# Three norms of a two-block transformer kernel: tile by tile, half by half, and the indexer weights turned afterwards

## The reference

```python
xn = _rmsnorm(x, mix_norm)
lru_x, lru_gate, q, k, v, qi, ki, wi, gate_a, gate_b = _split_cols(xn @ w_in)
ya = (rg_lru(causal_dwconv(lru_x)) * gelu(lru_gate)) @ w_lru_br
wih = wi * (IDX_HEADS ** -0.5)        # 8 indexer weights per token
score = einsum('bth,bths->bts', wih, relu(dots(qi, ki)))
yb = attention(q, k, v, top 64 keys of score, rel_bias) @ w_attn_br
x = x + (sigmoid(gate_a) * ya + sigmoid(gate_b) * yb) @ w_out
xn = _rmsnorm(x, ffn_norm)
x = x + (gelu(causal_dwconv(xn @ w_up[:, :D_FF])) * (xn @ w_up[:, D_FF:])) @ w_down
g_ple = sigmoid(_rmsnorm(x, ple_norm) @ w_ple_gate)
x = x + g_ple * (p @ w_ple_proj)
```

## Time and profile before

| | us |
|---|---|
| runs, median (lowest to highest of 3) | 1819.99 (1817.11 to 1826.1) |
| the profiled execution, its own time | 1821.22 |
| its span, first to last instruction | 1819.5 |
| PE busy | 1431.4 (79% of the span) |
| POOL busy | 612.7 (34%) |
| ACT busy | 442.8 (24%) |
| DVE busy | 421.3 (23%) |
| mean granted clock of TensorE | 0.917 of full |

### The profile page before, as it was taken

One profiled execution on the slowest core, in us unless ns is written; L12 is line 12 of the kernel. 1 busy time (PEld: TensorE's weight loads), 2 busy tenths in 40 slices (PEclk: granted clock), 3 DMA queues, 4 the chain that ended last, 5 costly groups with the idle time before them and its releaser, 6 DMA issues.

```text
span 1819.5 us, 21776 instructions
## 1 busy us (share of the span) xinstructions
PE 1431.4 (79%) x9218; PEld 983.6 (54%) x9218; DVE 421.3 (23%) x883; ACT 442.8 (24%) x538; POOL 612.7 (34%) x493
## 2 busy tenths in 40 slices
PE   7999998776567657765766677565899899899997
PEld 7899985333133213321332133121798888799985
DVE  3994542000000000000000000001317444233202
ACT  3445631000000000000000000001347453544333
POOL 6895870000000000000000000002386958688892
PEclk9999998898898889888998889888799899899998
DMA  9353467999999999999999999999155343355550
GB/s 351 139 186 140 174 232 269 406 409 410 410 409 410 410 409 410 410 409 409 410 410 409 410 410 409 410 410 417 62 180 193 123 162 139 139 186 186 185 185 24
DMA packets 116579, 539.45 MB, mean 296 GB/s; under 512 B 4440, under 2 KB 8544, under 8 KB 108832
## 3 DMA queue, kind: packets, MB, share of 16 engines
q1 hardware_dynamic: 113232, 532.44, 74.9%
q0 software_dynamic: 1184, 3.94, 0.6%
q10 hardware_dynamic: 2096, 2.11, 0.4%
HBM read 537.41 MB, written 1.06 MB: 296 GB/s over the span
## 4 chain that ended last, share of the span: by engine, by line
PE 44%; DMA 41%; SPq 6%; DVE 3%; ACT 3%; POOL 2%; issue 1%; DVEq 0%; ACTq 0%
DMA ring<-in_w 40%; PE bank L562 35%; SPq L384 6%; PE bank L782 6%; POOL ring_parts L499 2%; ACT ring_parts L1027 1%; DVE rows_parts L1803 1%; PE bank L768 0%; DMA ring<-in_units 0%; PE bank L695 0%; DVE slab L1830 0%; PE bank L740 0%; PE bank L817 0%; PE bank L959 0%; ACT slab L1187 0%
## 5 line engine op out<-in xcount | busy, mean ns | idle before, releaser
L499 POOL TENSOR_TENSOR ring_parts<-ring,ring_parts 128x512 fp32r<-128x512 f32 x456 | 598.6, 1351 | 160.7 <-ACT ring_parts L1027 160.7
L782 PE MATMUL bank<-ring,slab 128*32 128x512 f32 x2016 | 335.5, 801 | 291.7 <-DMA ring<-in_w 290.8
L562 PE MATMUL bank<-slab_parts,ring_parts 128*128 128x256 f32 x3328 | 500.8, 285 | 10.9 <-POOL ring_parts L499 8.4
L562 PEld LDWEIGHTS bank<-slab_parts,ring_parts 128*128 128x128 f32 x3328 | 460.0, 194 | 15.5 <-POOL ring_parts L499 8.8
L782 PEld LDWEIGHTS bank<-ring,slab 128*32 128x32 f32 x2016 | 66.3, 133 | 560.1 <-DMA ring<-in_w 371.5
L514 POOL TENSOR_TENSOR slab_parts<-slab,slab_parts 128x1088 fp32r<-128x1088 f32 x1 | 2.5, 2485 | 946.1 <-ACT slab_parts L1177 946.1
L1027 ACT ACTIVATE ring_parts<-ring 128x2048 fp32r<-128x2048 f32 x114 | 211.9, 1911 | 201.1 <-PE bank L562 201.1
L562 PE MATMUL bank<-rows_parts,ring_parts 128*128 128x256 f32 x752 | 188.6, 287 | 0.0
L562 PE MATMUL bank<-ring_parts,slab_parts 128*128 128x512 f32 (+1 forms) x672 | 162.3, 392 | 11.1 <-issue 5.2
L1737 DVE TENSOR_TENSOR slab<-slab,bank 128x512 f32<-128x512 f32 x16 | 11.0, 687 | 611.3 <-PE bank L782 611.3
L562 PEld LDWEIGHTS bank<-ring_parts,slab_parts 128*128 128x128 f32 x672 | 127.7, 192 | 38.7 <-issue 5.9
(11 more groups left out here) (289 smaller groups left out, 851.3 us busy)
## 6 DMA issues: line engine op xcount, KB each, us to landing
ring<-in_w SPq DMA_DIRECT2D x190, 2048.0 KB, 23.6
ring<-in_units SPq DMA_DIRECT2D x59, 2048.0 KB, 7.9
slab<-in_w SPq DMA_DIRECT2D x2, 2048.0 KB, 12.1
ring<-in_units SPq DMA_DIRECT2D x2, 1024.0 KB, 8.9
slab<-bias_scratch ACTq DMA_DIRECT2D x2, 1024.0 KB, 5.7
slab<-in_xT SPq DMA_DIRECT2D x1, 1024.0 KB, 5.2
rows<-in_ln_g POOLq DMA_DIRECT2D x2, 512.0 KB, 16.4
slab<-in_x SPq DMA_DIRECT2D x1, 1024.0 KB, 5.1
```

The costliest lines, as they stand in the source:

```text
L499: ins = g.tensor_tensor(r32(w_q), w_q, r32(high_q), ALU.subtract)
L562: return mm(out_, l, r, start=start and first, stop=stop and last)
L782: last = mm(b[CAP * j:CAP * j + CAP, :], xg[:, c, CAP * j:CAP * j + CAP], wt[:, j, i, :], start=c == 0, stop=c == DC - 1, tile_position=(0 ...
```

## The change

1. **Half-wise norms.** Square, scale and turning go by halves of 512 columns (`rms_square`, `rms_scale`, `turn_normed`), each with its own semaphore count. The two half sums are not added: DVE turns the first into the bias of the root (`rms_shifted`: sum/D + 1e-6), and the root adds the second (`rms_root`).
2. **x2.** DVE starts the layer norm of tile 0 when its two banks are combined (`tile_combined`), writes the centred values back to the banks and x from there by halves (`last_norm`), and puts the steps of tile 0's RMS norm between the statistics of tile 1. Tile 1 is scaled by DVE. `relb` goes ahead of the turning.
3. **Indexer weights.** The weight block of 8 columns becomes the stationary side, with 256 tokens streaming (24 products). The result is 8 rows; ACT writes them to `wi_rows`, and after `lx3` PE turns them back with two small transposes (task `wi`), which ACT copies between the copies of `lg_1` and `lg_3`.
4. **x3.** PE turns tile 0 between `mo0_1` and `mo1_1`. ACT runs tile 0's norm ahead of the copy of `fg0_1`, whose two halves stand in the gaps.
5. **x4.** The sums of the first half are made during the down products; tile 0's norm follows `dn1_0`; PE turns tile 0, runs two `pp` products, turns tile 1, runs the other two. The copy of `pg1_1` is split about the taking of tile 1.

```diff
-    n2 = [f"x2t{j}" for j in range(4)] + ["kiwi_k", "kiwi_w", "relb"]
-    n2 += [f"lx{j}" for j in range(4)] + [f"lg_{j}" for j in range(4)]
+    n2 = [f"x2t{j}" for j in range(4)] + ["relb", "kiwi_k", "kiwi_w"]
+    n2 += [f"lx{j}" for j in range(4)] + ["wi"] + [f"lg_{j}" for j in range(4)]
...
-    n2 += [f"yb{j}" for j in range(4)] + [f"mo{u}_{t}" for t in range(2) for u in range(2)]
-    n2 += [f"x3t{j}" for j in range(4)]
+    n2 += [f"yb{j}" for j in range(4)] + ["mo0_0", "mo1_0", "mo0_1", "x3t0", "x3t1", "mo1_1", "x3t2", "x3t3"]
...
-    n2 += [f"pp{u}_{t}" for u in range(2) for t in range(2)]
-    n2 += [f"x4t{j}" for j in range(4)]
+    for t in range(2):
+        n2 += [f"x4t{2 * t}", f"x4t{2 * t + 1}"] + [f"pp{u}_{t}" for u in range(2)]
...
+        def sum_count(stage, t, h):
+            return 4 * stage + (2 * h + t if stage == 2 else 2 * t + h) + 1
...
+                        if (u, t) in between:
+                            between[u, t]()
...
+            def turn_normed(src, pre, stage, t):
+                for k in range(2):
+                    pe.wait_ge(S("xn_half"), 4 * stage + 2 * t + k + 1)
+                    o = take_bank(f"{pre}t{2 * t + k}")
+                    for i in range(4):
+                        c = 4 * k + i
+                        last = nc.tensor.transpose(o[:, P * i:P * i + P], src[:, t, P * c:P * c + P], ident[:])
+                    full(last, f"{pre}t{2 * t + k}")
...
+                    if ends and t == 0:
+                        last.then_inc(S("tile_combined"), 1)
...
-            turn(tok(1), [f"x2t{j}" for j in range(4)], "xn_ready")
...
+            o = take_bank("relb")
+            full(mm(o[0:NH, 0:511], slab[0:NB, 9, 0:NH], slab[0:NB, 9, 16:16 + 511], start=True, stop=True), "relb")
+            for t in range(TT):
+                turn_normed(tok(1), "x2", 0, t)
...
-            for t in range(TT):
-                last = products(o[:, 8 * t:8 * t + 8], kiwi_parts, xn, True, slice(P, P + 8), slice(P * t, P * t + P), 0)
-            full(last, "kiwi_w")
...
+            full(products(o[0:IH, 0:T], kiwi_parts, xn, False, slice(P, P + IH), slice(0, T), 0), "kiwi_w")
...
+            wait_read(pe, "kiwi_w")
+            o = take_bank("wi")
+            for t in range(TT):
+                last = nc.tensor.transpose(o[:, IH * t:IH * t + IH], wi_rows[:, P * t:P * t + P], ident[0:IH, 0:IH])
+            full(last, "wi")
...
-            tile_by_tile([unit(1), unit(1)], merged2_parts, "mo", arrive=as_counted("merged2_low"))
-            turn(tok(4), [f"x3t{j}" for j in range(4)], "xn_ready", TT)
+            tile_by_tile([unit(1), unit(1)], merged2_parts, "mo", arrive=as_counted("merged2_low"),
+                         between={(1, 1): lambda: turn_normed(tok(4), "x3", 1, 0)})
+            turn_normed(tok(4), "x3", 1, 1)
...
+                turn_normed(tok(4), "x4", 2, t)
+                for u in range(2):
...
-            turn(tok(4), [f"x4t{j}" for j in range(4)], "xn_ready", 2 * TT)
...
-            def rms_tile(t, dst, done, at):
-                A(tok(dst)[:, t, :], tok(10)[:, t, :], ACT.Square, accum_out=small[:, at + t:at + t + 1]
+            def rms_square(stage, t, h):
+                cut = slice(512 * h, 512 * h + 512)
+                A(tok(4 if stage else 1)[:, t, cut], tok(10)[:, t, cut], ACT.Square, accum_out=square_sum(stage, t, h)
                   ).then_inc(S("rms_sum"), 1)
-                act.wait_ge(S("rms_sum"), done + t + 1)
-                A(small[:, at + 2 + t:at + 3 + t], small[:, at + t:at + t + 1], ACT.Sqrt, bias=eps_rms[:],
-                  scale=1.0 / D).then_inc(S("rms_root"), 1)
...
-                act.wait_ge(S("rms_inverse"), done + t + 1)
-                A(tok(dst)[:, t, :], tok(10)[:, t, :], ACT.Copy, scale=small[:, at + 2 + t:at + 3 + t]
-                  ).then_inc(S("xn_ready"), 1)
...
+            def rms_root(stage, t):
+                act.wait_ge(S("rms_sum"), sum_count(stage, t, 1))
+                act.wait_ge(S("rms_shift"), 2 * stage + t + 1)
+                A(rms_factor(stage, t), square_sum(stage, t, 1), ACT.Sqrt, bias=rms_shift(stage, t), scale=1.0 / D
+                  ).then_inc(S("rms_root"), 1)
+            def rms_scale(stage, t, h):
+                cut = slice(512 * h, 512 * h + 512)
+                act.wait_ge(S("rms_inverse"), 2 * stage + t + 1)
+                A(tok(4 if stage else 1)[:, t, cut], tok(10)[:, t, cut], ACT.Copy, scale=rms_factor(stage, t)
+                  ).then_inc(S("xn_half"), 1)
...
+            def rms_root(stage, t):
...
+            ln_root(0)
+            act.wait_ge(S("x2_ready"), 1)
+            rms_square(0, 0, 0)
+            act.wait_ge(S("x2_ready"), 2)
+            rms_square(0, 0, 1)
+            rms_root(0, 0)
+            rms_scale(0, 0, 0)
+            ln_root(1)
+            rms_scale(0, 0, 1)
+            take_turned("x2", [0], "mix_norm")
+            act.wait_ge(S("x2_ready"), 3)
+            rms_square(0, 1, 0)
+            act.wait_ge(S("x2_ready"), 4)
+            rms_square(0, 1, 1)
+            rms_root(0, 1)
+            take_turned("x2", [1, 2, 3], "mix_norm")
...
-            read(A(slab[:, 8, 1792:1808], o[:, 0:16], ACT.Copy, scale=IH ** -0.5), "kiwi_w")
+            read(A(wi_rows, o[0:IH, 0:T], ACT.Copy, scale=IH ** -0.5), "kiwi_w")
...
+            weights_high(1, "lg_1")
+            o = wait_full(act, "wi")
+            read(A(slab[:, 8, 1792:1808], o[:, 0:TT * IH], ACT.Copy), "wi")
+            weights_high(1, "lg_3")
...
-            weights_high(1, "fg0_1")
-            for t in range(TT):
-                wait_read(act, f"mo0_{t}", f"mo1_{t}")
-                rms_tile(t, 4, TT, 54)
-            take_turned([f"x3t{j}" for j in range(4)], "ffn_norm")
+            for h in range(2):
+                wait_read(act, f"mo{h}_0")
+                rms_square(1, 0, h)
+            rms_root(1, 0)
+            rms_scale(1, 0, 0)
+            rms_scale(1, 0, 1)
+            wait_read(act, "mo0_1")
+            rms_square(1, 1, 0)
+            take_turned("x3", [0, 1], "ffn_norm")
+            wait_landed(act, 1, "fg0_1")
+            wait_used(act, "mo0_1")
+            weights_high_half(1, "fg0_1", 0)
+            wait_read(act, "mo1_1")
+            rms_square(1, 1, 1)
+            rms_root(1, 1)
+            rms_scale(1, 1, 0)
+            rms_scale(1, 1, 1)
+            take_turned("x3", [2, 3], "ffn_norm")
+            weights_high_half(1, "fg0_1", 1)
...
-            weights_high(1, *down[2:])
-            weights_high(1, "pg0_1", "pg1_1")
-            for t in range(TT):
-                wait_read(act, f"dn0_{t}", f"dn1_{t}")
-                rms_tile(t, 4, 2 * TT, 62)
-            take_turned([f"x4t{j}" for j in range(4)], "ple_norm")
+            weights_high(1, *down[2:5])
+            for t in range(TT):
+                wait_read(act, f"dn0_{t}")
+                rms_square(2, t, 0)
+            weights_high(1, down[5], "pg0_1")
+            for t in range(TT):
+                wait_read(act, f"dn1_{t}")
+                rms_square(2, t, 1)
+                rms_root(2, t)
+                rms_scale(2, t, 0)
+                rms_scale(2, t, 1)
+                if t:
+                    wait_landed(act, 1, "pg1_1")
+                    wait_used(act, "dn1_1")
+                    weights_high_half(1, "pg1_1", 0)
+                take_turned("x4", [2 * t, 2 * t + 1], "ple_norm")
+            weights_high_half(1, "pg1_1", 1)
...
+            def rms_shifted(stage, t):
+                dve.wait_ge(S("rms_sum"), sum_count(stage, t, 0))
+                ts(rms_shift(stage, t), square_sum(stage, t, 0), 1.0 / D, 1e-6, ALU.mult, ALU.add
+                   ).then_inc(S("rms_shift"), 1)
...
+            def rms_inverse(stage, t):
+                dve.wait_ge(S("rms_root"), 2 * stage + t + 1)
+                v.reciprocal(rms_factor(stage, t), rms_factor(stage, t)).then_inc(S("rms_inverse"), 1)
...
+            def last_norm(t):
...
+                v.bn_stats(st[:, 0, :], acc[t][0][:]).then_inc(S("ln_bn"), 1)
+                if t:
+                    rms_shifted(0, 0)
+                v.bn_stats(st[:, 1, :], acc[t][1][:]).then_inc(S("ln_bn"), 1)
+                if t:
+                    rms_inverse(0, 0)
+                dve.wait_ge(S("ln_bn"), 2 * k + 2)
+                v.bn_aggr(small[:, 42 + 2 * t:44 + 2 * t], st).then_inc(S("ln_stats"), 1)
+                dve.wait_ge(S("ln_stats"), k + 1)
...
+                    stt(acc[t][u][:], acc[t][u][:], mean, rows[:, 1, cut], ALU.subtract, ALU.mult
+                        ).then_inc(S("ln_a"), 1)
...
+                    stt(tok(10)[:, t, cut], acc[t][u][:], rs, rows[:, 2, cut], ALU.mult, ALU.add
+                        ).then_inc(S("x2_ready"), 1)
...
+            dve.wait_ge(S("tile_combined"), 1)
+            last_norm(0)
             dve.wait_ge(S("combined"), GROUPS)
-            dve.wait_ge(S("ln2_landed"), 32)
...
+            last_norm(1)
...
+            rms_shifted(0, 1)
```

(33 more changed lines are left out.)

87 lines of the change are left out of this document (44 added, 43 removed).

## The result

| | before | changed |
|---|---|---|
| median of the runs | 1820.58 us (1817.11 to 1826.1, 4 runs) | 1795.82 us (1795.1 to 1799.48, 4 runs) |
| profiled execution, its span | 1821.22 us, 1819.5 us | 1795.1 us, 1793.4 us |
| mean granted clock over the span | 0.917 | 0.929 |

The ratio is 0.987, its 95% interval 0.985 to 0.989: 25 us faster. The forecast was 1796.0 us.

A forecast was written before the change was run, and what follows sets the result against it. Between long stretches of busy PE, three gaps where PE waits for a norm (x2, x3, x4) were taken as what could be won. 13.4 + 2.1 + 8.4 = 23.9 us off 1821.22 gave 1797.3, adjusted to 1796 for the median; range 1790 to 1803.

The forecast's parts named there:

- x2, start of `kiwi_k`: Gap at x2: half-wise norm steps let kiwi_k start at 1280.3 instead of 1285.94, 5.6 us earlier.
- x2, products behind: Behind the x2 gap: relb moved into idle time wins 1.8 us, the new form of indexer weights 5.0 us.
- The clock of `lx0` and the transposes of `wi`: Behind x2: lx0 at full clock wins 1.4 us; two small transposes of wi cost 0.4 us.
- The attention part, 0 us: Between x2 and x3: the 13.4 us won at x2 carries through to the end unchanged.
- x3, 2.1 us: Gap at x3: with tile 0 turned early, the next products start at 1567.2 instead of 1569.34, 2.1 us earlier.
- The clock survives x3: Rival at x3: PE's shorter idle pieces leave the clock up, 1.6 us more gained, 1794.5; chance 0.12.
- x4, 6.9 + 1.5 us: Gap at x4: pg starts 6.9 us earlier, and a clock that stays up wins 1.5 us in products.
- The fall behind 8-wide products: Rival at x2: clock falls, kiwi_w costs up to 2.2 us more and lx0 1.4 again, 1799.7; chance 0.17.
- The 3 us for hand-overs: Rival at x2 and x4: late hand-overs between engines shift what follows, 3 us more, 1799; chance 0.15.
- The gain was not given back: Rival before 1535 us: something in the attention part not following PE takes back x2's gain, 1809.5; chance 0.03.
- The supply of low parts: Rival in the feed-forward part: POOL and DVE in step slow 16 units by 2.7 us or more, 1840; chance 0.02.
- Does turning hold the clock?: Rival at x4: turnings count as idle, pg starts at half speed, the 1.5 us are lost, 1797.6; chance 0.08.

The follow-up runs named there:

- both_tiles: Changed kernel, but DVE begins the last layer norm only when both tiles are combined, not the first; 1797.66 us, ratio 0.989 to the kernel before.
- lx1_late: Changed kernel with ACT's high copy of lx1 moved behind the x2 norm, next to that of lx3; 1799.59 us, ratio 0.990 to the kernel before.
- high_first: Changed kernel with all high products of kiwi_k and fg0's first half ahead of those needing x's low part; 1797.83 us, ratio 0.989 to the kernel before.
- kiwi_tokens: Changed kernel with indexer weights again from 48 products streaming 8 columns, without task wi and its transposes; 1802.49 us, ratio 0.992 to the kernel before.
- fill_x3: Changed kernel plus four unread filler products at x3, two on either side of tile 1's turning; 1792.24 us, ratio 0.9855 to the kernel before.
- pp_first: Changed kernel with all pp products ahead of both x4 turnings, both tiles taken behind tile 1's scaling; 1805.29 us, ratio 0.993 to the kernel before.
- fill_both: Changed kernel plus four unread filler products at x3 and six at x2; 1795.75 us, ratio 0.987 to the kernel before.

## Why the prediction was right

It said 1796.0 and the range held it; the sum of 23.9 us was 26.1 in the profiled executions, and the difference of 2.2 is named below (0.50 of it lies ahead of x2, where the combine started earlier). That the median came out within 0.2 us of the forecast is luck: the medians differ by 24.8 us in one set of runs and by 22.8 in the other, and one term of the sum was off by 1.65. By the steps:

- **x2, start of `kiwi_k`, 5.6 us: right**, 5.47 once the 0.50 ahead of it is taken off. The bound was named rightly, ACT's table load (it ended at 1267.33; forecast 1267.85), and both_tiles shows it: DVE's start doesn't count, and lx1_late, where x was written 5.15 us behind the start of the combine once the copy was out of ACT's way, against 7.01. POOL was done when DVE scaled (at 1274.80, the scaling began at 1275.66), so of the price of a half, 0.35 to 1.2 us, the lower end held (0.88 us for two). One small step of DVE did wait for ACT beyond 1272, which the prediction had named as a sign of being wrong: 0.61 us, until 1274.35. It cost nothing against the sum, which already had ACT's squares of tile 1 end at 1275.75; they ended at 1274.93. A part of the 5.47 us is the clock's: before, the combine ran mostly at the low clock (5.86 us) and DVE waited for its end, while the changed kernel writes x 7.01 us behind its start with a combine of 3.67 us and 7.03 with one of 5.89 (high_first). By the rows of the kernel before I estimate that a combine of 3.67 us would have let it write x at 1268.3 and not 1270.33 (the root behind ACT's table load, 1267.85 + 0.29, would then be the bound), so that some 2.0 of the 5.47 us would be missing beside such an execution. No profile shows one.
- **x2, products behind, 1.8 + 5.0: right in sum**, 6.99 us. An 8-wide stationary side took 0.115 us a product at full clock, the price of the nearest row; a rate of 0.21 throughout was the other bound. The clock of `lx0` and the transposes of `wi`, +1.4 and -0.4: 1.06. All of x2: 13.5 against 13.4. kiwi_tokens gives the second part's share by itself, 6.6 of them.
- **The attention part, 0 us: wrong by 1.65.** The prediction said that the gain carries through unchanged. The products did, but the clock fell for a short while at 1433 and at 1477 in the profile before and not in the one after (the fall at 1419 before has its like at 1406 after). The one at 1433 began about 1 us behind the row of one-column products (1428.38 to 1431.84). Four of the later kernels lost 3 us and more in the same place. It comes and goes among kernels with the same products there, so I put it down to no part of the change; the term had no bounds of its own in my sum and should have had 3 us on either side.
- **x3, 2.1 us: 2.7 at the start of `fg0`, 1.8 at the end of the stretch.** Behind `mo1_1` it was 6.09 us (forecast 6.2), 3.6 less than the 9.68 before; the prediction's "4 us shorter" is 3.5 by its own times. The inserted turning was mis-sized, 0.87 us at full clock where I had 1.4. The rest went back: the clock rose only within 1556 to 1557, 5 to 6 us into `fg0`, where it was 3.6 before, and the stretch took 0.85 us longer. "The clock survives x3", a rival at 0.12, did not happen by itself; fill_x3 made it happen, and it was worth 2.4 us there (forecast 1.6).
- **x4, 6.9 + 1.5 us: right**, 6.97 and 1.65. PE did idle at its third turn, 0.45 us, waiting for ACT's scaling, but the turnings took 1.03 and 1.27 us and not 1.4, which paid for it.
- **The marks** that I had named: `kiwi_k` near 1280 (1279.97), `lx0` near 1288 at clock 1.00 (1287.19), `pg` behind the last `pp` (0.16 us idle). `fg0` 15.5 us earlier was 18.4. The table loads lay ahead of the ends of `mo0_1` and `dn1_1`. The late half of `fg0_1` ended no wait of PE.
- **The rivals.** The fall behind 8-wide products (0.17) is refuted: clock 1.00 through `kiwi_w`. The 3 us for hand-overs were not lost: `kiwi_k` and `pg` started within 0.2 us of their sums. The gain was not given back. The supply of low parts took 184.67 us of POOL in 206.22, against 179.83 in 205.50, and did not run into the bound.

**Does turning hold the clock?** At x4 it stayed at 1.00 over turning, `pp` and turning, and `pg` ran at full speed, so this rival fell. But the runs don't show that transpositions count. In pp_first both turnings (1.91 us) lie behind `pp`, which ends at 1762.06, and the clock fell within 1766 to 1767; at x3 in the changed kernel the last `mo` product ends at 1544.85, a turning of 1.27 us follows, and it fell within 1549 to 1550; where PE waits for POOL in the attention part, with nothing at all between, products end at 1401.66 and it fell within 1406 to 1407. The distance is 4 to 5 us each time. Over all profiles it varies, but in the same bounds whether turnings lie in it or not: 2.2 to 5.3 us at POOL's wait, 2.0 to 5.5 at x3, and 3.0 (before) and 4.3 (pp_first) at x4. The Trainium skill, "TensorE: Matmul & The Clock Gate", section "Part 4: PE-mode transpose", says that a transposition doesn't count as busy for the clock in the same way; these rows agree with it, but no run here has transpositions alone for longer, so they don't prove it. What held the clock at x4 were the `pp` products between, which pp_first took away.

## What to carry to other kernels

When a norm stands between two long runs of products, try independent products between the turnings of its tiles. At x4 that won 2.4 us of idle time and 2.7 in the clock of what comes behind; at x3, where one turning went between products that were there anyway, it won 0.9 us, and 0.4 by the end of the stretch behind, as the clock fell all the same. Make the small operand the stationary side and stream the wide one: in a row of 48 products that stream 8 columns the clock fell though TensorE was busy, and their followers ran at half speed too. And look at what ACT must load before its first root, since the engine that seems to wait (DVE here) may start earlier for nothing. Before an edit is given the credit for a few microseconds, look where the clock fell in both profiles.

## What the runs showed of the hardware

- 24 products with a stationary side of 8 columns and 256 streaming took 2.76 us at clock 1.00; 48 that stream 8 columns took 7.9 us (1284.26 to 1292.14), and the clock fell while they ran, with TensorE busy in every window.
- A clock that falls is low for long after work is back: in the changed kernel from within 1269 to 1270 to within 1283 to 1284 at x2, in kiwi_tokens from within 1286 to 1287 to within 1296 to 1297, with TensorE busy throughout the latter.
- Filler products hold it where they start before it falls (fill_x3, 2.4 us won); behind the fall they run at half speed themselves and delay what waits behind them, which at x2 took back what the earlier rise gave (fill_both: 1.3 us later, 1.5 won).
- Kernels with the same products in the same order differ by 3 us in one part of the program, by whether the clock falls once more there. Two profiles of one kernel, or marks on either side of that part, are needed before 3 us are put down to an edit.
